# Modulations: the weights become the stationary operand and the two conditioning vectors the moving columns

## The reference, cut to what matters

```python
D_MODEL, N_MOD = 1024, 6

def ada_mod(cv, w, b):
    m = jax.nn.silu(cv) @ w + b
    return jnp.split(m, N_MOD, axis=-1)
...
    for layer in range(DEPTH):
        sh1, sc1, g1, sh2, sc2, g2 = ada_mod(c[:, None, :], ada_w[layer], ada_b[layer])
        csh1, csc1, cg1, csh2, csc2, cg2 = ada_mod(c_ctx, ada_w[layer], ada_b[layer])
        h_lat = rmsnorm(x_lat, norm_mix[layer]) * (1 + sc1) + sh1
        h_ctx = rmsnorm(x_ctx, norm_mix[layer]) * (1 + csc1) + csh1
```

## Time and profile before

| what | value |
|---|---|
| median of 3 runs | 3738.14 us (3729.86 to 3749.73) |
| the profiled execution, its time | 3737.51 us |
| its span, first to last instruction | 3735.7 us |
| mean granted TensorE clock | 0.884 |
| TensorE matmul busy | 3033.4 us (81%), 13839 records |
| TensorE weight load busy | 2311.7 us (62%), 13839 records |
| VectorE, ScalarE busy | 1581.1 us (42%), 1211.6 us (32%) |
| the two `modulations` steps | from 30.3 and from 1502.4 us |

### The profile page before, as it was taken

How to read it: one execution, slowest core, us unless ns; L and a number is a source line. 1 busy time by engine, 2 the same in 40 slices (tenths; PEclk the granted TensorE clock), 3 DMA queues, 4 the chain that set the end, 5 groups by cost and what they waited for, 6 DMA issues and landing times. The chain is left out here.

```text
span 3735.7 us, 36904 instructions
## 1 busy us (share of the span) xinstructions
PE 3033.4 (81%) x13839; PEld 2311.7 (62%) x13839; DVE 1581.1 (42%) x2039; ACT 1211.6 (32%) x1592; POOL 128.0 (3%) x83
## 2 busy tenths in 40 slices
PE   6696787876999889866698799876965878589996
PEld 2283376664888777235477588755753646477775
DVE  1233331543233343022464344332236554478886
ACT  0220021323223232032232344233422332277775
POOL 0000000200000000000000000000000000112220
PEclk9897898887999999978899899988975779699998
DMA  6211011011111142711001222212210002379996
GB/s 243 83 52 60 17 45 45 1 45 57 56 67 60 53 125 76 263 40 30 23 1 40 73 101 79 84 40 73 81 39 0 1 19 72 154 298 349 350 335 247
DMA packets 71109, 362.51 MB, mean 97 GB/s; under 512 B 12852, under 2 KB 16771, under 8 KB 43876
## 3 DMA queue, kind: packets, MB, share of 16 engines
q1 hardware_dynamic: 64132, 352.85, 26.7%
q0 software_dynamic: 6880, 8.41, 0.6%
HBM read 360.68 MB, written 16.27 MB: 101 GB/s over the span
## 5 line engine op out<-in xcount | busy, mean ns | idle before, releaser
L281 PE MATMUL ps<-rounded,rounded 128*128 128x512 f32 (+3 forms) x3700 | 1403.5, 379 | 399.9 <-DVE rounded L266 260.3
L282 PE MATMUL ps<-rounded,rounded 128*128 128x512 f32 (+3 forms) x3700 | 1363.3, 368 | 0.0
L283 PE MATMUL ps<-rounded,rounded 128*128 128x512 f32 (+3 forms) x3700 | 1361.0, 368 | 0.0
L281 PEld LDWEIGHTS ps<-rounded,rounded 128*128 128x128 f32 (+1 forms) x3700 | 727.9, 197 | 581.0 <-DVE rounded L266 304.8
L283 PEld LDWEIGHTS ps<-rounded,rounded 128*128 128x128 f32 (+1 forms) x3700 | 728.9, 197 | 110.1
L282 PEld LDWEIGHTS ps<-rounded,rounded 128*128 128x128 f32 (+1 forms) x3700 | 731.8, 198 | 98.6
L266 DVE TENSOR_TENSOR rounded<-work,rounded 128x1024 fp32r<-128x1024 f32 (+3 forms) x224 | 306.9, 1371 | 1028.4 <-ACT rounded L262 1028.0
L262 ACT CAST rounded<-work 128x1024 fp32r<-128x1024 f32 (+3 forms) x224 | 261.1, 1166 | 764.5 <-PE ps L283 586.5
L2828 DVE TENSOR_TENSOR rounded<-work,rounded 128x2048 fp32r<-128x2048 f32 x138 | 311.7, 2288 | 92.5 <-ACT rounded L2676 89.8
L2676 ACT CAST rounded<-work 128x2048 fp32r<-128x2048 f32 x138 | 258.5, 1908 | 85.2 <-PE ps L283 85.2
L396 PE MATMUL ps<-work,silu_c 128*2 128x512 f32 x384 | 174.0, 607 | 24.6 <-DMA work<-in_ada_w 24.6
(11 more groups left out here) (413 smaller groups left out, 2452.4 us busy)
## 6 DMA issues: line engine op xcount, KB each, us to landing
work<-in_moe SPq DMA_DIRECT2D x138, 1024.0 KB, 7.0
work<-in_ada_w SPq DMA_DIRECT2D x24, 2048.0 KB, 8.1
work<-in_ffn_up SPq DMA_DIRECT2D x44, 1024.0 KB, 4.9
work<-in_ffn_down SPq DMA_DIRECT2D x66, 512.0 KB, 3.6
work<-in_w_out SPq DMA_DIRECT2D x16, 512.0 KB, 3.5
work<-in_w_gates SPq DMA_DIRECT2D x16, 512.0 KB, 3.4
work<-in_w_in_hy SPq DMA_DIRECT2D x12, 512.0 KB, 3.6
work<-in_hy_dft_lat SPq DMA_DIRECT2D x4, 1024.0 KB
```

The lines of the kernel that those rows point to most:

```text
L281: k.nc.tensor.matmul(out, sh, mh, start=start, stop=False)
L282: k.nc.tensor.matmul(out, sh, ml, start=False, stop=False)
L283: return k.nc.tensor.matmul(out, sl, mh, start=False, stop=stop)
```

## The change

The operands change places. For each of the 4 groups of 128 columns of a slot, and for each of the 8 input tiles, the 128 x 128 square of the weights is the stationary operand, and the two columns of `silu_c` move over it. The sums come out as `[128, 2]` columns, four groups of two columns side by side in the slot's bank. The copy of the two rows, the four turning matmuls, their constants and the semaphores `held` and `turned` go. VectorE's bias add reads the bank directly. The loads and their order stay.

```diff
-    rows = [k.arena[0:2, s * 512:(s + 1) * 512] for s in range(n)]
-    landed, done, held, turned, kept = ([k.sem(f"{w}{s}") for s in range(n)] for w in ("landed", "done", "held", "turned", "kept"))
+    landed, done, kept = ([k.sem(f"{w}{s}") for s in range(n)] for w in ("landed", "done", "kept"))
+
+    def sums(s, j):
+        return k.bank(s, 2, 2 * j)
+
...
                 for s in range(n):
                     pe.wait_ge(landed[s], 16 * i + 16)
                     pe.wait_ge(kept[s], i + 1)
-                    for kk in range(DT):
-                        last = nc.tensor.matmul(k.bank(s)[0:2, :], k.silu_c[:, kk, :], slots[s][:, kk * 512:(kk + 1) * 512],
-                                                start=kk == 0, stop=kk == DT - 1)
+                    for j in range(4):
+                        for kk in range(DT):
+                            at = kk * 512 + j * P
+                            last = nc.tensor.matmul(sums(s, j), slots[s][:, at:at + P], k.silu_c[:, kk, :],
+                                                    start=kk == 0, stop=kk == DT - 1)
                     last.then_inc(done[s], 1)
-                    pe.wait_ge(held[s], i + 1)
-                    for j in range(4):
-                        last = nc.tensor.matmul(k.bank(4 + s, 2, 2 * j), rows[s][:, j * P:(j + 1) * P],
-                                                k.cst[0:2, CAT["ident"]:CAT["ident"] + 2], start=True, stop=True)
-                    last.then_inc(turned[s], 1)
...
                 for s in range(n):
-                    dve.wait_ge(done[s], i + 1)
-                    nc.vector.tensor_copy(rows[s], k.bank(s)[0:2, :]).then_inc(held[s], 1)
-                    dve.wait_ge(turned[s], i + 1)
                     at = 4 * (i * n + s)
                     bias = k.vec[:, bass.ds(at + COL[f"ada_b_{layer}"], 4)].unsqueeze(2).to_broadcast([P, 4, 2])
-                    nc.vector.tensor_tensor(mod[:, bass.ds(at, 4), :],
-                                            k.bank(4 + s, 8).rearrange("p (j c) -> p j c", c=2), bias,
-                                            ALU.add).then_inc(kept[s], 1)
+                    dve.wait_ge(done[s], i + 1)
+                    nc.vector.tensor_tensor(mod[:, bass.ds(at, 4), :], k.bank(s, 8).rearrange("p (j c) -> p j c", c=2),
+                                            bias, ALU.add).then_inc(kept[s], 1)
```

## The result

The changed kernel takes 3852.28 us (median of 4 runs, 3845.43 to 3861.77) against 3737.91 us before (4 runs). The ratio is 1.0305 with a 95% interval of 1.0268 to 1.0342, so the change makes the kernel 3.0% slower, about 114 us.

The account below looks back on a forecast made before the run. TensorE's time per slot was taken to bound the two modulation stages. At clock 0.50, +56.2 and +56.6 us for the stages and +2 for the norms make +115 on 3738: 3853 us, 3.1% slower, range 3838 to 3872.

Parts of the forecast that it names:

- What bounds the steps: Both modulation stages: TensorE's own time for a slot, 8.78 us, decides; the DMA is waited for only at the first landing.
- The price of a pair: New matmul stream in both stages: each weight load with its matmul takes 214 ns at clock 0.50.
- The bounds of 205 and 230: Limits in ns for a two-column pair at clock 0.50: 7 us less or 12 us more a stage.
- The clock: Both modulation stages: granted clock stays at 0.50 throughout, as in the L2585 and L2592 streams; chance 88%.
- The sum: Whole kernel: 56.2 and 56.6 us more in the stages plus 2 for the norms, +115 us, giving 3853 us.
- the norms behind them: `normalise` after each stage: L458's 32 records begin at clock 0.50, costing about 1 us each, 2 in all.
- The rest of the kernel: Every stage other than those affected by the change: keeps its old length.
- The clock granted: Rival, both stages: 2.4 GHz comes after the first slot, a stage takes 91.5 us, kernel 3705 or 3694 us; chance 6%.
- the clock swinging: Rival, both stages: half of each at 1.00, pairs of 164 ns, +18 us each, 3776 us; chance 5%.

Follow-up runs that it names:

- wide turns first: Changed kernel with the first two of each stage's four turns at 128 moving columns, the last two at 2; 3766.47 us, one execution.
- cols128: Changed kernel with the two vectors repeated so each matmul moves 128 columns instead of 2; 3690.49 us, ratio 0.9872 to the kernel before.
- cols128_again: The changed kernel with 128 moving columns instead of 2, run again for comparison; 3683.78 us, ratio 0.985 to the kernel before.
- the hidden turning: Kernel before, with each slot's turning issued after the next slot's eight matmuls, operands unchanged; 3719.52 us, ratio 0.9955.

## Why the prediction was right

**What bounds the steps.** TensorE's own time for a slot, as said: 0.2 us of 164 idle, no wait for the DMA after the first landing.

**The price of a pair.** 214 ns was read from matmuls with 16 moving columns; those with 2 took 213.5. The bounds of 205 and 230 were not needed. The 108 ns read from L2585 at 1.00 counted records that cross the window's edges; the pairs measured at that clock take 112. The matmul records are 352 ns long, not 374, without effect, as they lie over each other, and the DMA moved 137 GB/s, not 150.

**The clock.** 0.50 throughout both steps, taken from L2585 and L2592. This was the step on which all hung, and the runs with 128 columns and with wide turns first show it as the cause, by changing nothing but the moving columns. In the Trainium skill, "TensorE: Matmul & The Clock Gate", section "LDWEIGHTS (loading the stationary operand)", the formula is the columns over 1.2 and names no clock. The estimate of 107 ns that follows for 128 columns is near the pairs at 1.00 (112 ns) and half of those at 0.50. The advice of the same page's section "Why this matters for your kernels", to keep TensorE busy without gaps, did not bring the high clock here: the stream was busy 163.99 of 164.20 us and stayed at 0.50.

**The sum.** Predicted were +56.2 and +56.6 us for the steps and 2 for the norms behind them. The steps measured +55.7 and +56.1. L457's 32 records took 12.88 us in the first norm and 13.31 in the second, 0.6 and 1.0 more than the 12.28 that they took in each before, for 1 forecast in each. By rows, the sum is thus 113.4 us and not 115; by the medians the difference is 114.4, and the prediction of 3853 is 0.7 us from the median of 3852.28. The close hit owes something to chance, since the four runs of either kernel spread over 16 to 20 us.

**The rest of the kernel.** I wrote that every other stage would have its old length. That step was wrong for the profiled pair. The spans differ by 118.7 us, 5.3 more than the steps and norms give. In layer 1's attention the same stretch of work took 14.7 us at 0.50 before and 8.8 us at 1.00 after; in the second block's mixer another took 25.6 us at 1.00 before and 38.8 us at 0.59 after. First the windows of before, then of after:

```profile
1866.50:1881.20 14.70, 14.70 (x49) 10.81 (x48) 6.69 (x12) 4.35 (x8) 0.00 (x0) 0.50 0.01 1
3026.40:3052.00 25.60, 23.54 (x136) 14.70 (x136) 12.79 (x23) 12.24 (x41) 0.00 (x0) 1.00 0.00 1
```

```profile
1973.60:1982.40 8.80, 8.06 (x46) 5.79 (x45) 5.58 (x10) 4.33 (x8) 0.00 (x0) 1.00 0.01 2
3129.20:3168.00 38.80, 37.80 (x139) 23.53 (x141) 13.04 (x23) 12.29 (x41) 0.00 (x0) 0.59 0.00 1
```

That such swings need no change of the kernel is shown by the two profiled executions of one and the same kernel, `cols128` and `cols128_again`. The attention stretch, somewhat longer here, from the same ScalarE instruction to the same, in the one and in the other:

```profile
1815.50:1829.10 13.60, 12.86 (x74) 9.47 (x73) 8.47 (x15) 6.01 (x11) 0.00 (x0) 1.00 0.01 1
```

```profile
1820.40:1843.30 22.90, 22.90 (x75) 17.06 (x74) 9.68 (x17) 6.15 (x11) 0.00 (x0) 0.50 0.00 1
```

13.6 us at a mean clock of 1.00 and 22.9 us at 0.50. That the swings between before and after are of this kind, and not set off by where the longer steps leave the clock, is argued from it and not shown.

**The rivals.** The clock granted (6%) and the clock swinging (5%) did not come. The first one's price was sound: where the clock is granted, by 128 columns, a step takes 88 to 89 us for the 91.5 of the rival's sum, and the measured 3684 to 3690 us lie just below the 3694 to 3705 that it gave.

## What to carry to other kernels

A matmul with a fresh square of weights did not become cheaper with fewer moving columns (213 ns with 64, 32 or 2 at 0.50; 112 ns with 128 or 2 at 1.00), and a stream of such matmuls without gaps, with 64 moving columns or fewer, was left at half the clock; so look in the trace for a stretch of the same kind and read its granted clock before swapping operands to save a transpose. Count loads as work of their own: the change removed 2 small steps a slot and multiplied the loads of 128 columns by eight (64 instead of 8), each at 213 ns. Where the moving columns don't set the pace, columns that are thrown away can be free, and here 126 of 128 useless ones made the kernel 162 us faster than the version without them, and 1.2 to 1.5% faster than the kernel before.

## What the runs showed that was not expected

- 64 moving columns with a load of 128 were still left at 0.50, at 13.65 us a slot, where 128 were granted 1.00 at 7.1 us. I had leaned the other way.
- The clock that was granted lasted for the first 4 us of the narrow stream, and was 0.50 from there to the end of the step, with TensorE never idle in between.
- Stretches whose granted clock is 1.00 in one execution and 0.50 to 0.59 in another, in the same code, are worth 6 to 13 us each. They are of the size of a whole edit here (18 us for the hidden turning), and a comparison of two profiles has to be made stretch by stretch.
